# A two-layer hybrid decoder trunk: all of mixers A and B woven into the attention, V before K at the start, a last projection in two passes, and masks by a minimum on VectorE

## The reference

```python
h = x @ w_in                       # z_a (u|v), z_b, q, k, v, gates (3 x 2048)
u, v = split(gelu(z_a)); v = layer_norm(v)
y_a = u * (causal w_sp applied within chunks of 128 tokens to v, + b_sp)
y_b = (trailing means over 2, 4, 8, 16 tokens of z_b, minus z_b) @ w_pool * pool_scale
y_c = attention: 8 heads of 128; a query sees its own block of 256 keys (causal)
      and the 3 past blocks with the largest q . mean(k); bias -slope[h] * (t - s)
mixed = sum_n sigmoid(gates_n) * (y_n @ w_branch_n)        # n = 0, 1, 2 for a, b, c
x = layer_norm(2**0.5 * x + mixed @ w_out)
ff = relu(x @ w_up)**2 @ w_down
ple = (p @ w_ple) * sigmoid(x @ w_ple_gate)
x = layer_norm(2**0.5 * x + ff + ple)
```

## Time and profile before

| | |
|---|---|
| runs | 8430.35, 8911.11, 10150.71 us |
| profiled execution | 8426.98 us |
| its span, slowest core | 8425.3 us |
| PE busy | 8197.5 us (97%), 40002 matmuls |
| DVE busy | 2872.1 us (34%) |
| ACT busy | 1457.9 us (17%) |
| DMA queue of POOL | 630.08 MB, 44.8% of the engines' span |

### The profile page before, as it was taken

How to read it: one execution, slowest core, us unless ns; L and a number is a source line. 1 busy time by engine, 2 the same in 40 slices (tenths; PEclk the granted TensorE clock), 3 DMA queues, 4 the chain that set the end, 5 groups by cost and what they waited for, 6 DMA issues and landing times.

```text
span 8425.3 us, 102751 instructions; the slowest of 8 cores (8416.1 to 8425.3 us)
## 1 busy us (share of the span) xinstructions
PE 8197.5 (97%) x40002; PEld 3793.8 (45%) x40002; DVE 2872.1 (34%) x3809; ACT 1457.9 (17%) x1736; POOL 682.8 (8%) x1269
## 2 busy tenths in 40 slices
PE   7999998899999999999999999989999999999996
PEld 3444444444444444444445444444444444444443
DVE  1342344533511134111444424355234111431116
ACT  0220123411200012000123101243011000110002
POOL 1000100000000010000100001000010000100000
PEclk9999999999999999999999999999999999999998
DMA  6444773245754457444674447633477444674443
GB/s 113 80 77 73 138 149 62 60 74 98 154 118 77 76 87 154 89 77 78 93 148 77 74 76 146 135 61 61 78 134 159 77 76 79 96 156 77 77 79 79
DMA packets 298907, 815.23 MB, mean 97 GB/s; under 512 B 78144, under 2 KB 94784, under 8 KB 298432
## 3 DMA queue, kind: packets, MB, share of 16 engines
q0 software_dynamic: 190352, 630.08, 44.8%
q1 hardware_dynamic: 108080, 178.58, 7.2%
HBM read 1354.66 MB, written 83.89 MB: 171 GB/s over the span
## 4 chain that ended last, share of the span: by engine, by line
PE 94%; DVE 2%; DMA 2%; issue 1%; ACT 1%; POOL 0%; DVEq 0%; ACTq 0%; POOLq 0%
PE ps L497 62%; PE ps L505 24%; PE ps L587 5%; PE ps L836 1%; PE ps L799 1%; DMA wb<-wstream 1%; DMA cb_bm<-c_bm 0%; ACT PT L808 0%; PE ps L530 0%; DVE oac L854 0%; DVE tmp L725 0%; PE ps L871 0%; DVE tmp L558 0%; DMA RX<-x2f 0%; PE ps L804 0%
## 5 line engine op out<-in xcount | busy, mean ns | idle before, releaser
L497 PE MATMUL ps<-RX,wb 128*128 128x512 bf16 x13312 | 2905.2, 380 | 47.0 <-DMA RX<-xT 38.4
L497 PE MATMUL ps<-RM,wb 128*128 128x512 bf16 x11264 | 2440.1, 379 | 1.1 <-DMA wb<-wstream 1.1
L497 PEld LDWEIGHTS ps<-RX,wb 128*128 128x128 bf16 x13312 | 1302.9, 98 | 1625.7 <-issue 74.1
L497 PEld LDWEIGHTS ps<-RM,wb 128*128 128x128 bf16 x11264 | 1102.1, 98 | 1331.0 <-issue 2.7
L505 PE MATMUL ps<-RX,wb 128*128 128x512 bf16 x6144 | 1394.4, 380 | 0.7 <-DVE P L958 0.7
L473 POOL DMA_DIRECT2D wb<-wstream x1188 | 630.7, 532 | 7582.3 <-PE ps L497 4063.7
L505 PEld LDWEIGHTS ps<-RX,wb 128*128 128x128 bf16 x6144 | 594.3, 98 | 684.4 <-issue 9.8
L991 DVE TENSOR_SCALAR tmp<-ps 128x1024 f32<-128x1024 f32 x256 | 313.6, 1225 | 1299.0 <-PE ps L497 1299.0
L505 PE MATMUL ps<-P,wb 128*128 128x512 bf16 x3072 | 704.7, 379 | 0.0
L1007 DVE TENSOR_TENSOR P<-P,ps 128x1024 f32<-128x1024 f32 x192 | 234.5, 1221 | 1091.5 <-PE ps L497 1091.5
L767 DVE SCALAR_TENSOR_TENSOR tmp<-tmp,ps 128x1024 f32<-128x1024 f32 x128 | 156.3, 1221 | 971.9 <-PE ps L505 971.9
(11 more groups left out here) (100 smaller groups left out, 3071.0 us busy)
## 6 DMA issues: line engine op xcount, KB each, us to landing
wb<-wstream POOLq DMA_DIRECT2D x1124, 512.0 KB, 5.1
x1f<-P SPq DMA_DIRECT2D x64, 512.0 KB, 8.8
tmp<-x1f SPq DMA_DIRECT2D x64, 512.0 KB, 18.2
tmp<-xT SPq DMA_DIRECT2D x32, 512.0 KB, 10.1
x2f<-P SPq DMA_DIRECT2D x32, 512.0 KB, 9.8
tmp<-x2f SPq DMA_DIRECT2D x32, 512.0 KB, 10.6
outT<-P SPq DMA_DIRECT2D x32, 512.0 KB, 3.6
RX<-xT POOLq DMA_DIRECT2D x16, 512.0 KB, 27.1
```

Source lines behind the costliest of these rows:

```text
L497: pe(lambda e, kc=kc, hf=hf: e.matmul(pr.t[:, hf * 512:(hf + 1) * 512], lhsT=wb.t[:, woff + kc * 128:woff + (kc + 1) * 128], rhs=act_fn(kc ...
```

## The change

Six things. (1) The weave holds, as fillers, branch 0, the pooling, the pool weights and branch 1: 228 filler steps instead of 96, over the same attention steps. Branch 2 stands alone behind it. The pooled result goes to the slot Y0, and the pool weights' result is written over it. (2) In a branch, the product of one output block comes after the gate product of the next. (3) Seven of the eight heads get the own block's mask by a minimum on DVE with a triangle of 3e38 and 0, after the exponential; their distance factor for the own block, formerly in the mask table, is a factor in the evacuation (`ownf`). Head 0 keeps the product. (4) In the first phase, V comes before K, and its first half takes x's channel blocks in order of arrival (`kfirst`); x comes in 16 transfers, with a weight unit before each four, and constants are `bg` jobs. (5) The last step's 16 "pg" units run twice, once for each 512 tokens (`pg_halves`); the first half's normalisation is dealt out during the second pass. A "pg" unit's two transfers have semaphores of their own. (6) All semaphores are cleared by one instruction with a range.

```diff
-    def branch(n):
+    def branch(n, mid=()):
         for dcp in range(8):
             u.append(("gate", n, 2 * dcp))
+            if dcp == 0:
+                u.extend(mid)
+            u.append(("gate", n, 2 * dcp + 1))
             u.append(("br", n, dcp))
-            u.append(("gate", n, 2 * dcp + 1))
 
     branch(0)
     for c in range(8):
         u.append(("pz", c))
+    branch(1, [("pw",)])
     branch(2)
-    u.append(("pw",))
-    branch(1)
     for dc in range(16):
         u.append(("wo", dc))
     return u
...
@@ -450,9 +456,13 @@
     unit_seq = []
     for l_ in range(DEPTH):
         for _s in range(NS):
-            unit_seq += [(l_, i) for i in range(NA)]
+            ks = list(range(NA))
+            if l_ == 0 and _s == 0:
+                ks = ks[8:16] + ks[0:8] + ks[16:]
+            unit_seq += [(l_, i) for i in ks]
         for _s in range(NS):
             unit_seq += [(l_, NA + i) for i in range(len(F_UNITS))]
+    unit_seq += unit_seq[-16:]
     wpos = {"dma": 0, "use": 0}
     in_wb = []
...
+                if kfirst and hf == 0:
+                    for k in range(4):
+                        for tc in range(8):
+                            tok_mm(wb, hf, k4, tc, k, x, xat)
...
-        tok_proj("av", x, xat, v_evac)
+        first = l == 0 and s == 0
+        if not first:
+            k_proj()
+        tok_proj("av", x, xat, v_evac, first)
+        if first:
+            k_proj()
...
+                if dc == 0 and mid is not None:
+                    yield from mid()
+                if dc % 2 == 1:
+                    wnew = nxt("br")
+                if prev is not None:
+                    if dc % 2 == 1:
+                        wbr = wnew
+                    yield from product(dc - 1, prev, wbr)
+                prev = sg
+            yield from product(15, prev, wbr)
...
-                       KV_ATOMS[j][0:1] + slot_atoms(0), Sat, inc=not own)
-                    if own:
+                       KV_ATOMS[j][0:1] + slot_atoms(0), Sat, inc=not (own and h == 0))
+                    if own and h == 0:
                         b0, bn = (0, 256) if par == 0 else (256, 128)
...
+                    if own and h > 0:
+                        dve(lambda e, a=a, PT=PT: e.tensor_tensor(out=PT.t[:, a:a + 128], in0=PT.t[:, a:a + 128], in1=cb["tri"].t[:], op=ALU.min),
+                            PT.a() + cb["tri"].a(), PT.a())
...
+                    if own and h > 0:
+                        m = cb["ownf"].t[:, h, qc % 2:qc % 2 + 1]
+                        own = False
...
+        def pool_steps():
+            for c in range(8):
+                wb = nxt("pz")
+                pr = next_pair()
+                yield from mm_pair_steps(wb, 0, 16, x, xat, pr, 4)
...
+        def pw_steps():
+            wb = nxt("pw")
+            for g in range(4):
...
+                yield
+
+        def fill_steps():
+            yield from br_steps(0, Y0, 1)
+            yield from pool_steps()
+            yield from br_steps(1, Y0, 1, pw_steps)
+
         nst = NH * sum(2 * (2 * s + hf) + 2 for hf in range(2))
         pairs[0] = PS[0:2]
-        interleave(att_steps(), 2 * nst + 1, br_steps(0, Y0, 1), 96)
+        interleave(att_steps(), 2 * nst + 1, fill_steps(), 228)
...
+    def pg_halves(x, XR):
+        s = NS - 1
+        for h in range(2):
+            hs = (h, h + 1)
+            cs = cols(hs)
+            for dc in range(16):
+                wb = nxt("pg")
+                pr = next_pair()
...
+                pg_evac(dc, hs, pr)
+                if h == 1:
+                    tick(1)
+            jobs = ln_jobs("ln2g", "ln2b", out_d, None, s, hs=hs)
+            if h == 0:
+                bg.extend(jobs)
+            else:
+                left = list(bg)
+                del bg[:]
+                bg.extend(jobs[1:2] + left + jobs[2:])
+
+    def pg_evac(dc, hs, pr):
+        cs = cols(hs)
+        sg, _ = next_tmp()
+        g = sg.t[:, 0:512]
+        act(lambda e: e.activation(out=g, in_=pr.t[:, 0:512], func=AF.Tanh, scale=0.5), pr.a(0), sg.a())
+        dve(lambda e: e.scalar_tensor_tensor(out=g, in0=g, scalar=1.0, in1=pr.t[:, 512:1024], op0=ALU.add, op1=ALU.mult), pr.a(1) + sg.a(), sg.a())
+        dve(lambda e: e.scalar_tensor_tensor(out=R(dc)[:, cs], in0=g, scalar=0.5, in1=R(dc)[:, cs], op0=ALU.mult, op1=ALU.add),
+            P.a(dc) + sg.a(), P.a(dc))
+        ln_acc(dc, hs)
...
-    w_dma()
-    for i in range(8):
-        load_x(0, 0, i, xT_d, None)
-        if i == 3:
+    for i in range(16):
+        if i % 4 == 0:
             w_dma()
-    for k, shp in CONST_SHAPES.items():
+        ch = sc.chan("x0_%d" % i)
+        cdma(lambda e, i=i: e.dma_start(out=RX[0].t[:, i, :], in_=xT_d[i * 128:(i + 1) * 128, 0:TS]), [], RX[0].a(i), ch)
...
-    for h in sc.sems:
-        nc.gpsimd.sem_clear(h)
+    nums = sorted(h.num for h in sc.sems)
+    assert nums == list(range(nums[0], nums[0] + len(nums)))
+    sem_range = range(nums[0], nums[0] + len(nums))
+    nc.gpsimd.sem_clear(sem_range)
```

More of the change, by code:

```diff
@@ L273, in build_consts @@
     c["akey"] = ak.astype(np.float32)
+    ow = np.zeros((128, 8, 2), dtype=np.float64)
+    for par in range(2):
+        ow[:, 1:, par] = np.exp((256.0 - 128 * par - p[:, None]) * slopes[None, 1:])
+    c["ownf"] = ow.astype(np.float32)
+    c["tri"] = np.where(s <= t, 3e38, 0.0).astype(np.float32)
     pn = np.zeros((128, 8, 8), dtype=np.float32)
@@ L345, in build_program @@
     TW = TS + 16
-    wbs = [sb("wb%d" % i, [128, PGSZ], BF16) for i in range(NWB)]
+    wbs = [sb("wb%d" % i, [128, PGSZ], BF16, 2) for i in range(NWB)]
     tmps = [sb("tmp%d" % i, [128, TW], F32) for i in range(NTMP)]
-    accs = sb("accs", [128, TS], F32, 1)
-    accq = sb("accq", [128, TS], F32, 1)
-    lnm = sb("lnm", [128, TS], F32, 1)
+    accs = sb("accs", [128, TS], F32, 2)
+    accq = sb("accq", [128, TS], F32, 2)
+    lnm = sb("lnm", [128, TS], F32, 2)
     PTs = [sb("PT%d" % i, [128, 512], BF16) for i in range(4)]
@@ L367, in build_program @@
     PS = [ps("ps%d" % i) for i in range(4)]
-    ch_wb = [sc.chan("wb%d" % i) for i in range(NWB)]
+    ch_wb = [[sc.chan("wb%d_%d" % (i, j)) for j in range(2)] for i in range(NWB)]
     ch_p = sc.chan("p")
@@ L470, in w_dma @@
         src = ws_d[l, off:off + 128 * n].rearrange("(p n) -> p n", p=128)
-        for o in range(0, n, USZ):
+        for j, o in enumerate(range(0, n, USZ)):
             m = min(USZ, n - o)
-            cdma(lambda e, o=o, m=m: e.dma_start(out=wb.t[:, o:o + m], in_=src[:, o:o + m]), [], wb.a(), ch_wb[wi])
+            cdma(lambda e, o=o, m=m: e.dma_start(out=wb.t[:, o:o + m], in_=src[:, o:o + m]), [], wb.a(j), ch_wb[wi][j])
         in_wb.append(wb)
@@ L576, in load_res, with tok_mm, tok_proj @@
         return tb
-    def tok_proj(kind, x, xat, evac):
+    def tok_mm(wb, hf, k4, tc, k, x, xat):
+        pr = PS[tc // 2]
+        bk = tc % 2
+        kc = 4 * k4 + k
+        pe(lambda e: e.matmul(pr.t[:, bk * 512:(bk + 1) * 512], lhsT=xtok(x, kc, tc), rhs=wb.t[:, k * 512:(k + 1) * 512],
+                              start=(kc == 0), stop=(kc == 15)),
+           wb.a(0) + xat(kc), pr.a(bk), inc=(kc == 15 or (tc == 7 and k == 3)))
+    def tok_proj(kind, x, xat, evac, kfirst=False):
         for hf in range(2):
@@ L585, in tok_proj @@
                     for k in range(4):
+                        if kfirst and hf == 0:
+                            continue
                         kc = 4 * k4 + k
@@ new lines, in pw_steps @@
+        def pw_steps():
+            wb = nxt("pw")
+            for g in range(4):
+                prs = []
+                for hh in range(2):
+                    pr = next_pair()
+                    prs.append(pr)
+                    for kc in range(2):
+                        for hf in range(2):
+                            o = g * 512 + kc * 256 + hh * 128
+                            pe(lambda e, o=o, g=g, kc=kc, hf=hf, pr=pr, wb=wb: e.matmul(pr.t[:, hf * 512:(hf + 1) * 512], lhsT=wb.t[:, o:o + 128],
+                                                                                       rhs=Y0[:, 2 * g + kc, hf * 512:(hf + 1) * 512],
+                                                                                       start=(kc == 0), stop=(kc == 1)),
+                               wb.a(0) + slot_atoms(1, 2 * g + kc), pr.a(hf), inc=(kc == 1))
+                for hh in range(2):
+                    cc = 2 * g + hh
+                    pr = prs[hh]
+                    dve(lambda e, cc=cc, pr=pr: e.tensor_scalar(out=Y0[:, cc, :], in0=pr.t[:], scalar1=lcb["pscale"].t[:, cc:cc + 1], scalar2=None,
+                                                                op0=ALU.mult), pr.a() + lcb["pscale"].a(), slot_atoms(1, cc))
+                yield
@@ L960, in phase_a @@
-        for _ in br_steps(1, Y0, 1):
+        for _ in br_steps(2, Y1, 2):
             pass
@@ L1009, in phase_f @@
```

(10 more changed lines are left out.)

207 lines of the change are left out of this document (102 added, 105 removed).

## The result

The changed kernel took 8317.46 and 8317.48 us in two of its six runs, the kernel before 8426.91, 8430.35 and 8435.87 in three of the six beside them: a ratio of **0.9865, 95% interval 0.9837 to 0.9894**, which at 2% counts as the same, though the sign is beyond doubt. In some executions of either kernel the cores of a die, or of both, show a lower granted clock and take longer (so the median of the six is 9138.87 us), and only dies without that are compared here. *Slowest core* is from here on the mean, over these dies of a kernel's runs, of each die's slowest core: 8432 us before (21 dies), 8317.0 after (8). The mean of the cores' spans went from 8427 to 8313 us. The forecast was 8296, with 8235 to 8375 as its range: right in kind, 21 us too good, and wrong in sign for one part, the end.

A forecast was written before the change was run, and what follows sets the result against it. PE, busy 97% of the span, was taken to bound the kernel. Masks 17, long weave 67, start 30 and end 17 sum to 131 us off 8427: 8296 us, range 8235 to 8375.

The forecast's parts named there:

- the end: Last projection in two passes: second pass at 4.5 us a block behind DVE, 184 us for 200.6, 17 us won.
- Doubled "pg" weights: Last projection: weights loaded twice as often, 590 KB per 3.89 us; counted as nothing, with 26 us as far end.
- rival D: Last passes held by transfers, each unit taking its 5.1 us landing time instead of 3.9; 26 us lost, 8322; 10%.
- The masks: Weaves: 28 of 32 mask products of each width go in each of four weaves, 17 us of PE work won.
- The long weave: Mixing stages: losses of 147 us fall to 80 as more fillers cover attention, 67 us won.
- the walk: Pooling bursts on DVE ahead of evacuations: block 6 costs 3 us, block 7 costs 1; 6 at s = 1, 3 at s = 0.
- plain items: Long weave at s = 1: 48 items lost 5 us at s = 0 before, so 112 lose 11.
- The start: First phase: clearing gives 5.9 us, x complete at 50, V's halves done at 52 and 80; 30 us won, between 18 and 37.
- B: Rival for the weave: the fillers buy nothing net, losses stay 147 us; 8363; 14%.
- C: Rival for weave, start and end: all is hidden, 187 us won; 8240; 19%.
- E: Rival for the weave: DVE's order holds PE through every burst, losses of 272 us for 147; 8488, slower; 4%.
- A: The forecast itself for the whole kernel: 8296 us, own range 8260 to 8335; 53%.

The follow-up runs named there:

- e1_scale_late: Changed kernel with ScalarE's scaling of the first half's normalisation, in its last pass, recorded one block later; slowest core 8298.9 us, 18 less.
- e7_one_add: Changed kernel with only the first of each run of pooling additions on VectorE done, sums left unfinished; slowest core 8283.6 us, 33 less.
- e10_clear_only: Kernel before with only the semaphores cleared by one range at both ends; slowest core 8422.5 us, mean of the cores 8418.6 for 8427.2.

## Why the prediction was right, and where it failed

- **The step that failed is the end:** "In the second PE needs 3.89 us a block, but DVE has four evacuations of 512 columns and, in 12 blocks, two steps of the first half's normalisation", 4.5 us. It counted each engine's work and took the fullest. Measured: 6.0 us a block with DVE idle in each, a ring between two engines that work in the order of the code; the second pass took 97.7 us, not 78. +8 instead of -17, and this is more than the whole error of the sum. Shown by e1_scale_late, where a block takes 4.37, the pass 79 and 18 us come back. Even so the end is 189 us, not 184; what follows the pass takes 48 for 44.
- **Doubled "pg" weights cost nothing:** as forecast. The first pass ran 62.26 us with PE at 61.94 while the DMA engines were busy 0.93, and PE never waited for `wb`. These transfers took 6.3 us (median) from issue to landing, as the line of their issues in the two passes has it:

```profile
DMA to landing us min/median/max: 5.0/6.3/10.5
```

That is more than the 5.1 of the earlier trace rows and than the 3.9 between two units, yet nothing waited, in e1_scale_late's second pass at 4.37 us a block neither: several are under way at once, and rival D's rule, one after the other at its landing time, is refuted. The Trainium skill (HBM Reference, Specifications) gave room for it with its 358 GB/s for a core. The trace agrees: it counts 147 GB/s in that window, in bf16, which is 294 GB/s read as float32 (an estimate), without a stall.
- **The masks:** -17 forecast, -11 to -13 in the stages and -15 in the span in the long weave. A minimum took 0.223 us (below), less than the 0.29 taken. What the prediction did not see is that the gain hangs on the other part of the change: alone it is nothing.
- **The long weave:** -67 forecast; -80 in the stages. It was mis-sized in two places that cancel in part. The bursts cost 33 us (e7_one_add) where the walk gave 18: it looked for the `yq` behind block 6 (3 us; found, 3.5), and not for "pw" behind block 7 (5.9). The plain items must then have cost less than the 0.1 us each that s = 0 had shown; this follows from the sum, and no run takes them by themselves. The new order of gate and branch product, put at nothing, cost 11 us in the short weave. Stages came out at 507 and 448 for the two weaves, for 513 and 445.
- **The start:** -30 forecast, -24.6 found: 17 from the order, 3.5 from the clearing, 4.2 from the small mask table, for which the prediction had only "less 2 for the constants that now come later". x was complete at 53.5 us, not 50. V's halves ended at 57.8 and 85.6, not 52 and 80: the term for two more units ahead of x's last block, "6 us, less 2", was too small, and a weight unit came 2.4 us late.
- **The rivals:** B (nothing bought), C (187 us off, all hidden) and E (slower) are each farther from the measured 8317 than A, and in the stages too: 91 us were won, for 84 in A and 124 in C. D's 8322 is nearer than A's 8296, but by luck: it lost 26 us to transfers in the last passes, and PE never waited for one there; the ring happened to cost as much. A's own range, 8260 to 8335, holds the result, by a slack that the end used up.

## What to carry to other kernels

When two in-order engines hand work to each other within an iteration, add up the ring, not only each engine's load: if an engine idles in every iteration and another waits for it, look for an instruction that stands ahead of the one needed and record it an iteration later. A cheap operation on a second engine saved the first engine's time here only where other work covered its latency, so measure such an edit beside the one that gives the cover. And read a wait by the order of the engine waited for: the line named may only be what stood behind a burst.

## What the runs showed of the hardware

The minimum on VectorE, by groups of the changed kernel (busy, mean ns, idle before):

```profile
L863 DVE TENSOR_TENSOR PT<-PT,cb_tri 128x128 bf16<-128x128 bf16 x224 | 47.4, 223 | 124.8 <-ACT PT L859 123.2 <-issue 0.2
```

223 ns is between the 0.29 taken from rows and the 0.13 estimated in the prediction. That estimate rests on two elements per cycle, from the Trainium skill (VectorE: DVE Perf Modes, the perf-mode tier table), and on the fixed term of 58 cycles in the same page's formula; the page adds that the measured fixed term is about 150 cycles, which gives 0.22 us (an estimate), and this trace agrees. Two that stand together take 0.35 us for both in 28 cases, so there a part overlaps, and 0.48 in 32.

One clear by range took the place of 68: in e10_clear_only the first transfer moved from 7.56 us (mean of the cores) to 2.23, 0.08 us for each clear left out, and the end became 4.7 us shorter. In the changed kernel the two are 5.1 and 3.4.

In the same run the first product came 5.3 us earlier and the first mixing stage only 3.5.

The mask table's transfers, issued by POOL and each waiting for the one before, held up all that POOL had to issue behind them: 37.6 us in the kernel before, of which PE felt 3 to 8 us, depending on the core.
